# Inverting 64x64 diagonal blocks in the delta rule, and a new order of turns, copies and combinations in the expert pairs

## The reference, cut to what matters

```
A = jnp.where(strict, jnp.einsum('bnhtd,bnhsd->bnhts', kb, kc) * L, 0.0)
T = lax.linalg.triangular_solve(eye + A, eye, left_side=True, lower=True, unit_diagonal=True)
U = T @ (vc * bc[..., None])
def step(state, inp):
    v_new = u - w @ state
    o = qd @ state + qkc @ v_new
    state = gl[..., None, None] * state + jnp.swapaxes(kd, -1, -2) @ v_new
```

```
xs = jax.vmap(lambda hb, ib: hb[ib])(h, idx)
a = silu(einsum('becd,edf->becf', xs, w_gate)) * einsum('becd,edf->becf', xs, w_up)
out = einsum('becf,efd->becd', a, w_down) * gate[..., None]
return zeros((n, Dm)).at[idx].add(out)
```

## Time and profile before

| | us |
|---|---|
| median of three runs | 3473.8 (3472.28 to 3484.75) |
| the profiled execution | 3486.42, of which span 3484.6 |
| TensorE busy | 3113.0 (89%) |
| VectorE busy | 1155.4 (33%) |
| ScalarE busy | 896.8 (26%) |
| mean DMA rate | 183 GB/s |

### The profile page before, as it was taken

How to read it: one execution, slowest core, us unless ns; L and a number is a source line. 1 busy time by engine, 2 the same in 40 slices (tenths; PEclk the granted TensorE clock), 3 DMA queues, 4 the chain that set the end, 5 groups by cost and what they waited for, 6 DMA issues and landing times. The chain is left out here.

```text
span 3484.6 us, 39509 instructions
## 1 busy us (share of the span) xinstructions
PE 3113.0 (89%) x17446; PEld 2112.2 (61%) x17446; DVE 1155.4 (33%) x1616; ACT 896.8 (26%) x1354; POOL 0.2 (0%) x4
## 2 busy tenths in 40 slices
PE   5997889999898788999989998879899985999997
PEld 3775767888676576788867766644343352443442
DVE  3446533233445653323343236630000136100002
ACT  3443223222444312322243350220000032100001
POOL 0000000000000000000000000000000000000000
PEclk8997989999999798999999999889999997999999
DMA  7224312322223411232363106249999952799996
GB/s 256 80 90 147 97 37 85 97 91 91 76 85 109 168 39 40 93 97 91 100 216 122 37 3 240 73 152 404 409 408 409 409 193 93 301 409 409 409 408 242
DMA packets 247386, 637.14 MB, mean 183 GB/s; under 512 B 12848, under 2 KB 110128, under 8 KB 247088
## 3 DMA queue, kind: packets, MB, share of 16 engines
q1 hardware_dynamic: 244128, 627.22, 48.4%
q10 hardware_dynamic: 3088, 7.40, 0.6%
HBM read 632.48 MB, written 2.10 MB: 182 GB/s over the span
## 5 line engine op out<-in xcount | busy, mean ns | idle before, releaser
L609 PE MATMUL ps<-mix_halves,work_halves 128*128 128x512 f32 (+1 forms) x1544 | 623.5, 404 | 39.5 <-DVE h_halves L2095 30.3
L609 PE MATMUL ps<-h_halves,work_halves 128*128 128x512 f32 (+1 forms) x1544 | 610.1, 395 | 4.6 <-DVE mix_halves L2095 2.4
L609 PE MATMUL ps<-mix_halves,ring_halves 128*128 128x512 f32 x1448 | 568.1, 392 | 0.0
L2095 DVE TENSOR_TENSOR ring_halves<-ring,work_halves 128x2048 fp32r<-128x2048 f32 (+2 forms) x125 | 252.6, 2021 | 546.2 <-ACT work_halves L1488 449.3
L609 PE MATMUL ps<-ring,work 128*64 128x512 f32 x1680 | 389.4, 594 | 22.3 <-DMA ring<-in_w_exp_gate 18.3
L609 PEld LDWEIGHTS ps<-mix_halves,work_halves 128*128 128x128 f32 (+1 forms) x1544 | 291.8, 189 | 126.7 <-issue 42.6
L609 PEld LDWEIGHTS ps<-h_halves,work_halves 128*128 128x128 f32 (+1 forms) x1544 | 292.5, 189 | 72.5 <-issue 6.4
L609 PEld LDWEIGHTS ps<-mix_halves,ring_halves 128*128 128x128 f32 x1448 | 272.3, 188 | 60.7
L1488 ACT ACTIVATE work_halves<-ring 128x2048 fp32r<-128x2048 f32 x102 | 188.3, 1846 | 425.6 <-PE ps L609 333.2
L609 PEld LDWEIGHTS ps<-ring,work 128*64 128x64 f32 x1680 | 128.0, 137 | 256.0 <-issue 255.6
L2474 DVE SCALAR_TENSOR_TENSOR x<-ps,small,x 128x512 f32<-128x512 f32 x112 | 82.3, 750 | 594.3 <-PE ps L609 592.8
(11 more groups left out here) (371 smaller groups left out, 3349.3 us busy)
## 6 DMA issues: line engine op xcount, KB each, us to landing
ring<-in_w_exp_gate SPq DMA_DIRECT2D x114, 1024.0 KB, 11.3
ring<-in_w_exp_down SPq DMA_DIRECT2D x100, 1024.0 KB, 12.8
ring<-in_w_exp_up SPq DMA_DIRECT2D x96, 1024.0 KB, 15.1
ring<-in_ada_w SPq DMA_DIRECT2D x48, 1024.0 KB, 7.4
ring<-in_w_mod SPq DMA_DIRECT2D x48, 1024.0 KB, 7.5
proj<-in_w_exp_up SPq DMA_DIRECT2D x28, 1024.0 KB, 12.8
proj<-in_w_exp_down SPq DMA_DIRECT2D x28, 1024.0 KB, 16.0
ring<-in_w_in SPq DMA_DIRECT2D x22, 1024.0 KB, 5.4
```

What stands on the lines that cost most here:

```text
L609: i = pe.matmul(o, lhsT, rhs, start=start, stop=stop, **kw)
L2095: to("lo", tt(rounded(v), v, rounded(hi), ALU.subtract))
```

## The change

In the delta rule the levels now run on the 64x64 diagonal blocks alone. `g_Ac`, `g_Tc`, `g_Yc` and `g_Xc` hold sixteen systems as 128x64: the block of tokens 0 to 63 in partitions 0 to 63, that of tokens 64 to 127 below it. A product is two matmuls of 64x64x64 for each system, `lower` and `upper`, which write the same bank in different partitions. Levels 2 to 32 are five rounds of this; the level of 64 becomes one product of the off-diagonal block (`g_Ar`) with the first block's T and one with the second block's Y, 16 matmuls each. The full Y is put together by two copies, a multiplication by -1 and a fill of zeros. Masks are the compact ones that an earlier stage already makes. Copies and subtractions go by halves (eight systems) instead of heads, so that a level has two copies and four subtractions. Modulation vector 5 moves behind the first two chunks of the recurrence, its turn behind the third, its columns behind the loop.

```diff
-                for hd in range(H1):
-                    for c in range(NT):
-                        turn(ps[:, hd, c * P:c * P + P], g_Y[:, hd, c * P:c * P + P], "g_t" if c == NT - 1 else None)
+                def products(bank, lhs, rhs, half, signal):
+                    for g in blocks(half):
+                        for r in (lower, upper):
+                            mm(at_block(r, bank, g), lhs[r, g, :], rhs[r, g, :], True, True,
+                               signal if g % 8 == 7 and r is upper else None)
...
+                for n in range(len(LEVELS) - 2):
+                    for half in range(2):
+                        pe.wait_ge(*due("g_al"))
+                        if n:
+                            pe.wait_ge(*due("g_tt"))
+                        products(0, g_al[n % 2], g_Tc, half, "g_x")
+                    if n == 0:
+                        pe.wait_ge(*due("gn"))
+                        pe.wait_ge(*due("mod_ready"))
+                    for half in range(2):
+                        pe.wait_ge(*due("g_x_sb"))
+                        if n:
+                            pe.wait_ge(*due("g_yt"))
+                        products(6, g_Yc, g_Xc, half, "g_dt")
+                        products(4, g_Xc, g_Yc, half, "g_dy")
...
+                    if c < 2:
+                        mod_panels(PLANS[f"layer{l}"], 5, 2 * c, 5)
+                    if c == 2:
+                        mod_turn(5, 5)
...
-                link(tt(by16(g_A), by16(g_A), const("below").unsqueeze(1).to_broadcast([P, 16, P]), ALU.mult))
-                link(tt(by16(g_Y), by16(g_A), table(first_t, "level1").unsqueeze(1).to_broadcast([P, 16, P]), ALU.mult))
-                to("g_y", tt(by16(g_Y), ident.unsqueeze(1).to_broadcast([P, 16, P]), by16(g_Y), ALU.subtract))
+                dve.wait_ge(*due("g_diag"))
+                link(tt(g_Yc, g_Ac, b_mask[:, 6:7, :].to_broadcast([P, 16, 64]), ALU.mult))
+                to("g_y", tt(g_Yc, b_mask[:, 0:1, :].to_broadcast([P, 16, 64]), g_Yc, ALU.subtract))
...
+                dve.tensor_copy(g_Yq[0:64, :, 0, :], g_Yc[0:64, :, :])
+                dve.tensor_copy(g_Yq[64:P, :, 1, :], g_Yc[64:P, :, :])
+                for half in range(2):
+                    dve.wait_ge(*due("g_dy"))
+                    to("g_yt", ts(g_Yq[0:64, eight_of(half), 1, :], change(4, half)[0:64, :, :], -1.0, None, ALU.mult))
```

```diff
-                     5: (range(3, 5), range(0, 4)), 6: (range(3, 5), range(4, 8)), 7: (range(5, 7), range(0, 4))}
+                     5: (range(3, 5), range(0, 4)), 6: (range(3, 5), range(4, 8)), 7: (range(5, 7), range(0, 8))}
...
+                    for m in blocks[:2]:
+                        combine(sources, m, 6 + m % 2)
+                    for bank in (2, 3):
+                        claim(bank)
                     pair(2, x_sel, "e_up")
-                    if p == 7:
-                        combine_blocks(range(5, 7), range(4, 8))
+                    if p in gate_tiles:
+                        turn_gates(4)
+                        pe.wait_ge(*due("r_pgT_sb"))
...
+                    for m in blocks[2:-2]:
+                        combine(sources, m, 6 + m % 2)
                     pe.wait_ge(*due("e_act"))
...
+                    for m in blocks[-2:]:
+                        combine(sources, m, 2 + m % 2)
-                    pair(4, e_actT, "e_down")
+                    pair(4, e_actT, "e_down", (0, 2), "aT_sb")
```

More of the change, by code:

```diff
@@ L247 @@
     "g_kb": "VectorE: k beta", "g_k": "TensorE: k by tokens", "g_k_sb": "ScalarE: in SBUF",
+    "g_diag": "ScalarE: the lower diagonal blocks beside the upper ones",
     "g_score": "TensorE: a head's products", "g_acc": "VectorE: with decay", "g_y": "VectorE: the first level's inverse",
@@ L964, in delta @@
                 pe.wait_ge(*due("g_k_sb"))
[L965 to L967 removed]
+                for first in (0, 2):
+                    mod_panels(PLANS[f"layer{l}"], 4, first, 4, (4,))
                 pe.wait_ge(*due("g_y"))
[L969 to L971 removed]
+                lower, upper = slice(0, 64), slice(64, P)
@@ new lines, in at_block, with blocks @@
+                def at_block(rows, bank, g):
+                    return ps[rows, bank + g // 8, g % 8 * 64:g % 8 * 64 + 64]
+                def blocks(half):
+                    return range(8 * half, 8 * half + 8)
+                def products(bank, lhs, rhs, half, signal):
[3 more added lines that the diff above has]
+                               signal if g % 8 == 7 and r is upper else None)
@@ L972, in delta @@
+                for g in range(16):
+                    for r in (lower, upper):
+                        t = pe.matmul(at_block(r, 0, g), g_Yc[r, g, :], ident[r, r], start=True, stop=True)
+                        if g % 8 == 7 and r is upper:
+                            t.then_inc(sem["g_t"], 1)
                 mod_turn(4, 4)
[L973 to L976, removed]
+                pe.wait_ge(*due("g_t_sb", 2))
@@ L996, in delta @@
-                        if not last:
-                            if n == half == 0:
-                                pe.wait_ge(*due("gn"))
-                            for hd in (2 * half, 2 * half + 1):
-                                if half:
-                                    pe.wait_ge(*due("g_tt"))
-                                for c in range(NT):
-                                    cs = slice(c * P, c * P + P)
-                                    mm(ps[:, 6 + hd % 2, cs], g_Y[:, hd, cs], g_X[:, hd, cs], True, True,
-                                       "g_dt" if c == NT - 1 else None)
@@ L1006, in delta @@
-                    pe.wait_ge(*due("g_yt", 2))
-                    if not last:
-                        pe.wait_ge(*due("g_tt", 2))
+                        pe.wait_ge(*due("g_x_sb"))
[4 more added lines that the diff above has]
+                for half in range(2):
+                    pe.wait_ge(*due("g_tt"))
+                    for g in blocks(half):
+                        mm(at_block(upper, 0, g), g_Ar[lower, g, :], g_Tc[lower, g, :], True, True,
+                           "g_x" if g % 8 == 7 else None)
@@ L1009, in delta @@
+                for half in range(2):
+                    pe.wait_ge(*due("g_x_sb"))
+                    pe.wait_ge(*due("g_yt"))
+                    for g in blocks(half):
+                        mm(at_block(lower, 4, g), g_Xc[upper, g, :], g_Yc[upper, g, :], True, True,
+                           "g_dy" if g % 8 == 7 else None)
+                pe.wait_ge(*due("g_yt", 2))
                 for c in range(NT):
```

189 lines of the change are left out of this document (98 added, 91 removed).

## The result

| | before | after |
|---|---|---|
| median | 3477.24 us (3472.28 to 3484.75, 4 runs) | 3378.55 us (3374.73 to 3387.84, 4 runs) |
| profiled execution | 3486.42 | 3378.0, of which span 3376.1 |
| TensorE busy | 3113.0 | 3032.8 |

What follows compares the result with a forecast made beforehand. TensorE was taken to bound the delta rule's levels, VectorE the work ahead of them, DMA the experts. Delta rule -87 (39.5 + 5.1 - 1.2 a layer) and experts +4 gave -83: 3473.8 to 3391 us, range 3366 to 3422.

Steps and rivals of the forecast that it cites:

- The levels: Delta rule inversion, second product to recurrence: TensorE alone sets each level at 6.5 us; 36.8 instead of 76.3, -39.5 a layer.
- the half product: In the levels, eight systems or 16 matmuls in two quarters: 8 x 0.135 = 1.08 us.
- 1 us for a slow clock at the start: Allowance in the levels' sum for a slow start at the lower clock, 1 us a layer.
- The run-up: Ahead of the levels: VectorE loses operations and stays last, -5.1 us a layer.
- The moved vector: Vector 5's matmuls, moved into the recurrence, cost more than TensorE's idle time there: +1.2 us a layer.
- uncertainty of -5: Recurrence clock: added matmuls might keep it at 1.00 or not, between -5 and +2 us.
- SyncE's queue and the ring: Four panels released 55 us later in the delta rule cost nothing, as the ring's DMA is then idle.
- The experts: Pair 7: with two blocks only, up meets its last two panels' waits; +1.9 us a stage, +4 for both.
- (a): Levels: two quarters writing one bank take turns, half a product 2.16, a level 13.0 us; total 3456; chance 8%.
- (b): Levels: small matmuls let the clock fall to 0.50, a level 13 us; total about 3456 to 3465; chance 7%.
- (c): Levels: quarters drain for each other, half a product 4 us, a level 24; total 3578; chance 4%.
- (d): Levels: diagonal quarters run faster, 0.54 a half, VectorE last at 4.0 a level; total 3366; chance 5%.

Runs made afterwards that it cites:

- e5_held_panels: Modulation vector 5 ahead of the levels, against the changed kernel, plus SyncE holding the eight freed panels until the levels are over; median 3401.15 us, ratio to before 0.9773.
- e4_vector_ahead: Against the changed kernel, modulation vector 5 goes back ahead of the levels; median 3401.13 us, ratio to before 0.9784.
- e12_both: Against the changed kernel, vector 5's panels placed two before the recurrence, one behind chunks 0 and 1 each; pair 7 with four blocks before up; 3363.66 us, ratio 0.9677.
- e3_one_quarter: Against the changed kernel, each half product's eight lower-quarter matmuls all come before the eight upper ones instead of alternating; 3477.69 us, one run.

## Why the prediction was right, step by step

**The levels: right in mechanism, the half product was over-sized.** The step said 1.08 us, read from the length of the score rows; it is 0.93. That a quarter's pace doesn't depend on its neighbours was right: its records start 58 ns apart with one, two or four quarters in use. The reading was wrong: 1.09 us from the first score to the next shape has 0.16 of start and change in it, and of the x32 row's 1.15 the step took off 0.07 for the end, where the last record alone stands 0.22. With 0.93 the prediction's own sum comes out 4.8 us a layer lower and is right to the tenth: 32 halves x 0.93 + 1.3 for the end of the last level = 31.1, and e5_held_panels measured 31.1 in both layers. The step's 1 us for a slow clock at the start was near for the second layer, where the first level's halves took 1.6, 1.7 and 1.1 us before they came to 0.93, and wrong for the first.

**What the sum had no term for** is the hole of 1.43 us. With it and 0.8 of smaller delays the stretch is 33.3 instead of 31.1; forecast 36.8. (The second layer has no hole and loses as much by the clock: 33.5.) That the panels' transfers slow TensorE here is shown: the holes came with eight panels in flight, were fewer and shorter with four, and vanished with none. That they do it by way of the instructions is shown as far as packets can: each of the ten holes ends 1.3 to 1.5 us behind a packet of instructions, and these packets come 6.7 us apart while eight panels load and 3.8 us apart otherwise. What makes them late, the order of the queues or something else, stays open.

**The run-up was right.** From the stage's start to the second product it was 4.8 and 4.9 us less (-5.1 forecast), with VectorE's columns last, as said.

**The moved vector: wrong sign; this is the step that failed.** The prediction took +1.2 from the idle 1.17 us and left the clock as an uncertainty of -5. The clock was the main effect: -1.8 and -4.3 us in the two recurrences, and -1.6 and -2.5 in the projections behind them, for which the sum had no term. The comparison that it should have made, moved or not moved within the new levels, is larger still: e4_vector_ahead shows 5.4 and 5.9 us more for the recurrences, 2.1 and 1.5 for the projections, and holes of 7.0 us a layer where after has 1.43 and none. I had looked for what the four freed panels cost SyncE's queue and the ring, and found nothing; what their transfers do to TensorE's instructions I didn't ask.

**The experts were right**, +2.6 and +2.1 for +1.9, by the waits that were named: up's last two panels. e12_both undoes exactly what the step blamed, and the waits are gone in the second stage; in the first one of 0.8 us is left.

**The rivals.** (a), quarters taking turns in one bank, is refuted by e3_one_quarter: alternating gives 0.93 where one after the other gives 1.51. The Trainium skill ("TensorEngine Tiling (Array Packing)", Gotcha 1) says that different row tiles cannot access the same PSUM bank at the same time. As far as the pace shows, here they do, in different partitions of it: each quarter's records keep the 58 ns that they have when it works alone, and the variant that writes the two to different banks is no faster (1.91 us for two halves against 1.89). (b), a falling clock in the levels, did not happen to after but for 3.4 us at the start of the second layer's; it did in full to e3_one_quarter. (c) and (d) find nothing in the rows: half a product is neither 4 nor 0.54.

Added up, the touched stages gave 101 us where 83 were forecast: 3.5 and 3.3 more from the levels, 3.0 and 5.5 from the recurrences, 1.6 and 2.5 from the projections, less 0.5 for the run-ups and 1 for the experts. The medians differ by 98.7; the 2 us between are within the scatter of the other stages. The time itself was off by less (12), since before's median came out 3.4 higher in the later runs.

## What to carry to other kernels

When matmuls get small, count instructions as a transfer: here their packets share the DMA engines with the weights, so time panel loads away from the bursts, but not so late that the next step waits. Filler that is needed anyway belongs into TensorE's idle time right at a seam, where the clock would fall; moving 1.93 us of it there shortened the stage by 2.9 and 2.5, of which 1.6 came back in one of the projections. Take a pace from what repeats, start to start, and not from the length of a row: the length has the start, the end and the change to the next shape in it, 0.16 of 1.09 us here.

## What the runs showed of the hardware that was not expected

- TensorE's clock stayed at 0.50 with TensorE recorded busy for 74.00 of 74.00 us, when the matmuls used one 64x64 quarter after the other; with the same matmuls in two quarters by turns it was 1.00 in the first layer, and 1.00 again after 3.4 us in the second.
- The records of float32 64x64x64 matmuls in one quarter of the array start 58 ns apart at a clock of 1.00 and 107 ns apart at 0.50, with one quarter in use (the last level), two that share columns or don't, or four. A matmul has two records, so it takes 0.117 us in its quarter, and two quarters together make one every 0.058 us. Eight matmuls in one quarter followed by eight in the other start 0.75 us apart, less than their 0.93, since the next group begins while the last three records of the one before still start.
- TensorE stood still for up to 2.85 us at a time without any semaphore while weights loaded at a DMA share of 1.10, and not at all in the levels when these transfers were held back. Each time it went on 1.3 to 1.5 us behind the end of a packet of 16,384 bytes of instructions, and such packets came 6.7 us apart instead of 3.8.
